# Dilated attention scores over 128 rows, h kept in DRAM meanwhile, three of eight probability units scaled on VectorE

## What is computed

```python
h = h + 0.5 * swiglu(rms_norm(h, ffn1_norm), ffn1_w1, ffn1_w3, ffn1_w2)
u = rms_norm(h, mix_norm)
proj = u @ w_in                       # q, k, v of 12 heads of 64; 4 pools; 2 gates
q, k = apply_partial_rope(q), apply_partial_rope(k)
for g, (window, dilation) in enumerate(((128, 1), (512, 4), (2048, 16))):   # 4 heads each
    s = (q @ k.T) * 64 ** -0.5        # banded, causal
    p = exp(s - max(s)); l = sum(p); o = p @ v / l; lse = max(s) + log(l)
o = sum(softmax(lse over the 3 groups) * o)
merged = gates[0] * (o @ w_branch_attn) + gates[1] * (pooled(proj) @ w_branch_pool)
h = h + merged @ w_out
h = h + 0.5 * swiglu(rms_norm(h, ffn2_norm), ...)      # then the retention and stick-breaking layers
```

## Time and profile before

| | |
|---|---|
| median of 3 runs | 1864.92 us (1864.58 to 1866.64) |
| profiled execution, its own time | 1866.13 us |
| span of that execution, first to last instruction | 1864.1 us |
| TensorE busy | 1850.0 us (99%), 10799 matmuls |
| weight loads (PEld) busy | 1627.6 us (87%) |
| VectorE busy | 1324.1 us (71%) |
| ACT busy | 890.8 us (48%) |
| POOL busy | 61.7 us (3%) |
| mean granted TensorE clock | 0.998 of full |
| DMA | 212.55 MB, mean 114 GB/s |

### The profile page before, as it was taken

One profiled execution on the slowest core, in us unless ns is written; L12 is line 12 of the kernel. 1 busy time (PEld: TensorE's weight loads), 2 busy tenths in 40 slices (PEclk: granted clock), 3 DMA queues, 4 the chain that ended last, 5 costly groups with the idle time before them and its releaser, 6 DMA issues.

```text
span 1864.1 us, 27146 instructions
## 1 busy us (share of the span) xinstructions
PE 1850.0 (99%) x10799; PEld 1627.6 (87%) x10799; DVE 1324.1 (71%) x1786; ACT 890.8 (48%) x1182; POOL 61.7 (3%) x80
## 2 busy tenths in 40 slices
PE   9999999999999999999999999999999999999997
PEld 7998998888889988989998888888888888888886
DVE  8875887887678889856888745463646776666666
ACT  6652664436365536634653342433336644444445
POOL 0000000010000000000000000000000000000000
PEclk9999999999999999999999999999999999999999
DMA  6744763341216426654753222122221222212213
GB/s 214 184 124 125 196 171 101 132 125 69 74 55 176 141 98 163 169 161 123 193 151 112 102 81 101 68 90 72 105 84 56 91 84 75 90 69 89 90 68 91
DMA packets 49633, 212.55 MB, mean 114 GB/s; under 512 B 5648, under 2 KB 8240, under 8 KB 38144
## 3 DMA queue, kind: packets, MB, share of 16 engines
q1 hardware_dynamic: 38816, 178.80, 28.1%
q0 software_dynamic: 10288, 31.84, 9.0%
q10 hardware_dynamic: 432, 0.56, 0.1%
HBM read 203.32 MB, written 3.67 MB: 111 GB/s over the span
## 4 chain that ended last, share of the span: by engine, by line
PE 94%; DVE 3%; ACT 1%; issue 1%; DMA 0%; DVEq 0%; ACTq 0%
PE acc L2419 20%; PE acc L2420 20%; PE acc L2421 20%; PE acc L2425 7%; PE acc L2426 7%; PE acc L2427 7%; PE att L2420 2%; PE att L2421 2%; PE att L2419 2%; PE att L2425 1%; PE att L2427 1%; PE att L2426 1%; PE acc L2683 1%; PE acc L2658 1%; DVE w_lo L1350 0%
## 5 line engine op out<-in xcount | busy, mean ns | idle before, releaser
L1350 DVE TENSOR_TENSOR w_lo<-raw,w_hi 128x2048 fp32r<-128x2048 f32 (+1 forms) x120 | 271.4, 2262 | 69.8 <-ACT w_hi L642 68.9
L642 ACT ACTIVATE w_hi<-raw 128x2048 fp32r<-128x2048 f32 (+1 forms) x120 | 226.5, 1888 | 120.4 <-PE acc L2421 105.6
L2419 PE MATMUL acc<-x_hi,w_hi 128*128 128x512 f32 x712 | 280.3, 394 | 0.3 <-DVE tmp L1578 0.3
L2421 PE MATMUL acc<-x_hi,w_lo 128*128 128x512 f32 x712 | 277.4, 390 | 0.0
L2420 PE MATMUL acc<-x_lo,w_hi 128*128 128x512 f32 x712 | 277.3, 389 | 0.0
L2419 PEld LDWEIGHTS acc<-x_hi,w_hi 128*128 128x128 f32 x712 | 133.7, 188 | 30.9 <-issue 2.7
L2420 PEld LDWEIGHTS acc<-x_lo,w_hi 128*128 128x128 f32 x712 | 133.7, 188 | 28.4 <-issue 1.2
L2421 PEld LDWEIGHTS acc<-x_hi,w_lo 128*128 128x128 f32 x712 | 133.6, 188 | 28.0
L2425 PE MATMUL acc<-xt_hi,w_hi 128*128 128x256 f32 x516 | 144.6, 280 | 0.0
L2427 PE MATMUL acc<-xt_hi,w_lo 128*128 128x256 f32 x516 | 144.3, 280 | 0.0
L2426 PE MATMUL acc<-xt_lo,w_hi 128*128 128x256 f32 x516 | 144.3, 280 | 0.0
(11 more groups left out here) (477 smaller groups left out, 4665.4 us busy)
## 6 DMA issues: line engine op xcount, KB each, us to landing
raw<-in_ret_head SPq DMA_DIRECT2D x24, 1024.0 KB, 4.8
raw<-in_ffn_down SPq DMA_DIRECT2D x32, 704.0 KB, 4.1
raw_c<-in_ffn_seven SPq DMA_DIRECT2D x37, 512.0 KB, 5.3
raw<-in_ffn_seven SPq DMA_DIRECT2D x33, 512.0 KB, 4.7
raw<-in_ffn_seven POOLq DMA_DIRECT2D x33, 512.0 KB, 7.5
raw<-in_ffn_seven SPq DMA_DIRECT2D x37, 256.0 KB, 4.5
raw<-in_ret_out SPq DMA_DIRECT2D x8, 1024.0 KB, 4.7
raw<-in_sb_v SPq DMA_DIRECT2D x8, 1024.0 KB, 4.7
```

Source lines behind the costliest of these rows:

```text
L642: nc.scalar.activation(w_hi[:, slot, at:at + cols], raw[:, slot, 0:cols], ACT.Copy).then_inc(w_hi_ready, 1)
L1350: tt(w_lo[:, slot, at:at + cols], raw[:, slot, 0:cols], w_hi[:, slot, at:at + cols].bitcast(F32), ALU.subtract).then_inc(w_ready, 1)
L2419: mm(dst, still[0], move[0], start=first, stop=False)
L2421: return mm(dst, still[1], move[0], start=False, stop=last)
```

## The change

`h` is written to a DRAM tensor `h_parked` by SP once the first feed-forward part has finished it, and is read back in four DMAs on Pool's queue behind the first four `add_pair`. In between, its room of 16 KB per partition holds `k_rest[j]` (per head j of the pass: low key parts of all groups on the head's own rows, zeros on the others) and `q_low[0]`, `q_low[1]`; `q_low[2]` takes the room of `ssq`. `q_both` and `k_both` now have all three groups; `qk_hi` and `qk_lo` are gone. Each group is copied in halves of 64 rows, and each has four DMAs to the other rows, twelve per pass. A unit has eight matmuls, all over 128 rows: the two masks, and two for each group. `first_score` waits for all twelve DMAs and for the zeros, VectorE's first low half for the store of h, and VectorE before adding to h for the four loads. VectorE no longer waits for the first pass's DMAs before the pool rows. For units 3, 5 and 7 VectorE multiplies by the reciprocal, right after taking it, and ACT doesn't.

```diff
+VECTOR_SCALED = (3, 5, 7)
...
+        with ExitStack() as under:
+            k_rest = [sb(f"k_rest{j}", [P, N_GROUPS, TOK], F32R, under) for j in range(2)]
+            q_low = [sb(f"q_low{g}", [P, TOK], F32R, under) for g in range(N_GROUPS - 1)]
         h = sb("h", [P, DC, TOK])
+        h_parked = nc.dram_tensor("h_parked", (P, DC, TOK), F32, kind="Internal").ap()
...
@@ SP
             for g in range(N_GROUPS):
                 fetch(dram["mix_qk"][0, g])
+            sp.wait_ge(h_ready, DC)
+            sp.dma_start(h_parked, h[:]).then_inc(park_landed, 16)
             for i in range(2):
                 fetch(dram["mix_pool"][i])
@@ POOL
+            pool.wait_ge(park_landed, 16)
+            pool.wait_ge(seg_done, FFN_SEGS[0] + 1)
+            for j, rows in enumerate(head_rows[::-1]):
+                nc.gpsimd.memset(k_rest[j][rows, :, :].bitcast(F32), 0.0).then_inc(rest_clear, 1)
...
+                for g in range(N_GROUPS):
+                    done = 2 * (N_GROUPS * a + g)
+                    pool.wait_ge(both_ready, done + 1)
+                    for j in range(2):
+                        pool.dma_start(q_both[j][other[j], g, :], q_low[g][own[j], :]).then_inc(both_landed, 16)
+                    pool.wait_ge(both_ready, done + 2)
+                    for j in range(2):
+                        pool.dma_start(k_both[j][other[j], g, :], k_both[j][own[j], g, :]).then_inc(both_landed, 16)
...
                     v.next()
+                    if j < 3:
+                        pool.wait_ge(prob_ready, 2 * UNITS)
+                        rows = slice(2 * (2 * (j - 1) + k), 2 * (2 * (j - 1) + k) + 2)
+                        pool.dma_start(h[:, rows, :], h_parked[:, rows, :]).then_inc(h_back, 16)
@@ ACT
-                if g:
-                    ins = nc.scalar.activation(qk_hi[:, o, g - 1, :], t(o), ACT.Copy, scale=QK_SCALE[o])
-                else:
-                    for j, rows in enumerate(head_rows):
-                        ins = nc.scalar.activation((k_both if o else q_both)[j][rows, :], t(o)[rows, :], ACT.Copy, scale=QK_SCALE[o])
+                for j, rows in enumerate(head_rows):
+                    ins = nc.scalar.activation((k_both if o else q_both)[j][rows, g, :], t(o)[rows, :], ACT.Copy, scale=QK_SCALE[o])
...
-                act.wait_ge(rden_ready, inv.next())
+                inv.next()
+                if k in VECTOR_SCALED:
+                    return
+                act.wait_ge(rden_ready, inv.k)
@@ VectorE
-                if g:
-                    stt(qk_lo[:, o, g - 1, :], t(o), QK_SCALE[o], qk_hi[:, o, g - 1, :].bitcast(F32), ALU.mult, ALU.subtract).then_inc(op_ready, 1)
-                else:
-                    for j, rows in enumerate(head_rows):
...
+                if both.k == 0:
+                    dve.wait_ge(park_landed, 16)
+                for j, rows in enumerate(head_rows):
+                    dst, high = (k_rest[j][rows, g, :], k_both[j][rows, g, :]) if o else (q_low[g][rows, :], q_both[j][rows, g, :])
+                    stt(dst, t(o)[rows, :], QK_SCALE[o], high.bitcast(F32),
+                        ALU.mult, ALU.subtract).then_inc(both_ready if j else op_ready, 1)
+                dve.wait_ge(both_ready, both.next())
...
                 nc.vector.reciprocal(rden[:, k:k + 1], den[:, k:k + 1]).then_inc(rden_ready, 1)
+                if k in VECTOR_SCALED:
+                    at = KEYS * (k % 3)
+                    dve.wait_ge(rden_ready, prob.k)
+                    nc.vector.tensor_scalar(tmp[:, at:at + KEYS], tmp[:, at:at + KEYS], rden[:, k:k + 1], None, ALU.mult).then_inc(vector_scaled, 1)
...
-            dve.wait_ge(both_landed, 4 * 16)
...
+            dve.wait_ge(h_back, 4 * 16)
@@ TensorE
-                mm(wide, both[:, plain[r]], keys[:], start=False, stop=False)
-                mm(wide, both[rows, plain[r]], k_low[rows, :], start=False, stop=True)
-                for g in range(N_GROUPS - 1):
-                    last = passes(narrow[:, P * g:P * (g + 1)], (q[0][:, g, :], q[1][:, g, :]),
-                                  (qk_hi[rows, 1, g, plain[r]], qk_lo[rows, 1, g, plain[r]]), False, g == N_GROUPS - 2)
+                q, high, rest = q_both[head], k_both[head], k_rest[head]
+                mm(wide, q[:, 0, plain[r]], high[:, 0, :], start=False, stop=False)
+                mm(wide, q[:, 0, plain[r]], rest[:, 0, :], start=False, stop=True)
+                for g in range(1, N_GROUPS):
+                    dst = narrow[:, P * (g - 1):P * g]
+                    mm(dst, q[:, g, plain[r]], high[:, g, plain[r]], start=False, stop=False)
+                    last = mm(dst, q[:, g, plain[r]], rest[:, g, plain[r]], start=False, stop=g == N_GROUPS - 1)
...
+                    if k in VECTOR_SCALED:
+                        pe.wait_ge(vector_scaled, by_vector.next())
+                    else:
+                        pe.wait_ge(scaled_ready, prob.next())
...
-                pe.wait_ge(both_landed, 4 * 16 * (a + 1))
+                pe.wait_ge(rest_clear, 2)
+                pe.wait_ge(both_landed, 4 * N_GROUPS * 16 * (a + 1))
```

More of the change, by code:

```diff
@@ L252, in block_kernel @@
             with ExitStack() as inner:
-                q_both = [sb(f"q_both{j}", [P, TOK], F32R, inner) for j in range(2)]
-                k_both = [sb(f"k_both{j}", [P, TOK], F32R, inner) for j in range(2)]
-                qk_hi = sb("qk_hi", [P, 2, N_GROUPS - 1, TOK], F32R, inner)
-                qk_lo = sb("qk_lo", [P, 2, N_GROUPS - 1, TOK], F32R, inner)
+                q_both = [sb(f"q_both{j}", [P, N_GROUPS, TOK], F32R, inner) for j in range(2)]
+                k_both = [sb(f"k_both{j}", [P, N_GROUPS, TOK], F32R, inner) for j in range(2)]
                 va = sb("va", [P, TB, N_GROUPS * GROUP_HEADS, 2, HEAD], F32R, inner)
@@ L408, in block_kernel @@
         both_landed = sem("both_landed")
+        park_landed = sem("park_landed")
+        rest_clear = sem("rest_clear")
+        h_back = sem("h_back")
         mix_copied = sem("mix_copied")
@@ L586, in _ @@
                 pool.dma_start(dst[:], dram[name]).then_inc(mix_landed, 16)
+            pool.wait_ge(park_landed, 16)
+            pool.wait_ge(seg_done, FFN_SEGS[0] + 1)
+            for j, rows in enumerate(head_rows[::-1]):
+                nc.gpsimd.memset(k_rest[j][rows, :, :].bitcast(F32), 0.0).then_inc(rest_clear, 1)
             def other_halves(a):
                 own, other = head_rows, head_rows[::-1]
-                pool.wait_ge(both_ready, 2 * a + 1)
-                for j in range(2):
-                    pool.dma_start(q_both[j][other[j], :], q_low[own[j], :]).then_inc(both_landed, 16)
-                pool.wait_ge(both_ready, 2 * a + 2)
-                for j in range(2):
-                    pool.dma_start(k_both[j][other[j], :], k_both[j][own[j], :]).then_inc(both_landed, 16)
+                for g in range(N_GROUPS):
[6 more added lines that the diff above has]
+                        pool.dma_start(k_both[j][other[j], g, :], k_both[j][own[j], g, :]).then_inc(both_landed, 16)
             other_halves(0)
@@ L1702, in rope_done @@
                 dve.wait_ge(hi_ready, hi.next())
-                if g:
-                    stt(qk_lo[:, o, g - 1, :], t(o), QK_SCALE[o], qk_hi[:, o, g - 1, :].bitcast(F32), ALU.mult, ALU.subtract).then_inc(op_ready, 1)
-                else:
-                    for j, rows in enumerate(head_rows):
-                        stt((k_low if o else q_low)[rows, :], t(o)[rows, :], QK_SCALE[o], (k_both if o else q_both)[j][rows, :].bitcast(F32),
-                            ALU.mult, ALU.subtract).then_inc(both_ready if j else op_ready, 1)
-                    dve.wait_ge(both_ready, both.next())
+                if both.k == 0:
[5 more added lines that the diff above has]
+                dve.wait_ge(both_ready, both.next())
                 op.next()
@@ L2631, in scores @@
             def scores(a, k):
-                r, rows = k // 2, slice(HEAD * (k % 2), HEAD * (k % 2) + HEAD)
+                r, head = divmod(k, 2)
                 if k >= 2:
```

11 lines of the change are left out of this document (3 added, 8 removed).

## The result

| | before | after |
|---|---|---|
| median of 4 runs | 1865.29 us (1864.58 to 1866.64) | 1882.55 us (1881.76 to 1883.38) |
| span of the profiled execution | 1864.1 us | 1881.6 us |
| TensorE busy | 1850.0 us | 1847.9 us |
| VectorE busy | 1324.1 us | 1334.1 us |

The changed kernel is slower: ratio 1.0092, 95% interval 1.0074 to 1.0109, or +17.3 us. 1875 with a range of 1868 to 1881 had been predicted: the sign was right, the size was not.

A forecast was written before the change was run, and what follows sets the result against it. TensorE, holding 94% of the chain, was taken to bound the kernel, with VectorE nearly abreast in the attention stage. Terms 4.0 - 0.6 + 8.9 - 1.2 - 0.9 = +10.2 us gave 1875 us, range 1868 to 1881.

The forecast's parts named there:

- the key transfers: Second pass, before the first score: both last-group key DMAs must land; two issues take 1.03 us, landing 2.3 us.
- first pass up to the first turn: Lengthened copies make TensorE 4.8 us later at the first value slab, two scores give back 0.8: +4.0 us.
- second pass up to the first score: Lengthened copies, then the last group's key DMAs, move the first score from 503.24 to 512.1: +8.9 us.
- rival a: Clock falls to 1.2 GHz in the wait before the second pass's first score: 3 to 5 us, 1877 to 1880; chance 0.3.
- The copies: Query and key copies of groups 1 and 2, halved: each 1.35 us longer, four times per pass over a head pair.
- the attend loops: VectorE decides the pace in each pass's loop: -0.6 us in the first, -0.9 in the second; bounds +0.3 and -2.0.
- The scaling: Attend loops, two of four rounds that split weights: VectorE takes 0.65 us per scaling, ACT gives up 0.83 us.
- The scores: TensorE saves 0.4 us a unit, at most 6.4 over 16 units; three before the second pass's first turn give -1.2.
- What was meant to be hidden: Store of h (6.7 us estimated), memsets and loads of h outside the attention stage's waits: priced at 0, to +1.5 us.
- (b): Copies shorter or better hidden, say by VectorE slack in the first pass: about +2.7 us, 1867.6; chance 0.14.
- (c): Scores count in full, everything else is covered by queued value blocks: -6.4 us, 1858.5; chance 0.05.
- (d): Scores over 128 rows of 128 columns take 0.2 us each, nothing saved: +13 us, 1878; chance 0.05.

The follow-up runs named there:

- e6_old_scores: Changed kernel with the ten score matmuls of before on the new tiles and all units scaled on ACT; 1884.53 us, ratio 1.0105.
- e2: Changed kernel with all eight units scaled on ACT again, none on VectorE; 1880.28 us, ratio 1.0080.
- e7_vector_halves: Kernel before with only VectorE's low parts of groups 1 and 2 in halves, ACT's copies whole; 1872.44 us, ratio 1.0035.
- e10b_early_keys: e8_reordered with each key transfer issued behind ACT's copy of its head instead of VectorE's last low part; 1874.23 us, ratio 1.0047.
- e8_reordered: Changed kernel, all scaling on ACT, scores of units 0 and 1 moved in both passes, useless matmuls before two rotations; 1874.30 us, ratio 1.0046.
- e1_keep_clock: Changed kernel with 53 useless matmuls in TensorE's four longest waits; 1878.41 us, ratio 1.0070.

## Why the prediction was wrong, step by step

Measured were +17.3 us instead of +10.2. Of the 7.1 us between them the clock is 4.1 to 4.5, the two attend loops 2.4 and the key transfers 0.4. The run with the clock kept shows the steps free of the clock, so its milestones are set against the terms of the sum.

| term | predicted | measured |
|---|---|---|
| first pass up to the first turn | +4.0 | +4.0 |
| loop of the first pass | -0.6 | +0.5 |
| second pass up to the first score | +8.9 | +9.3 |
| scores ahead of the first product | -1.2 | -1.2 |
| loop of the second pass | -0.9 | +0.4 |
| sum | +10.2 | +13.0 |
| clock | 0 (rival a: up to 5) | +4.1 of the medians, 4.5 between the two traces |

- **The copies: right.** The lengthenings of 1.35 us each gave 4.8 at the value slab, with 0.6 absorbed (measured 5.0), and 4.15 at the last rotation (measured 4.2). VectorE's halves alone gave half of that, and both engines' halves all of it. The +4.0 at the first turn was luck, though. I had TensorE arrive 4.8 later and win 0.8 by the scores; but filling TensorE's wait with scores moved nothing in the reordered kernel. With the clock kept, VectorE's weight split ahead of that turn starts 4.9 us later than before (430.88 instead of 425.97), and VectorE's idle time behind it shrinks from 2.31 us to 1.39: 4.9 less 0.9 is 4.0 as well. In the reordered kernel that idle time is 1.42. So the chain through VectorE's splits set the turn at the full clock; in the changed kernel, with the clock at 0.50, VectorE idled 3.07 us there, and TensorE set it.
- **The key transfers: right, 0.4 us too small.** I let the two issues follow at once (1.03 us for both the earlier trace rows); in the changed kernel they start 0.87 us apart instead of about 0.5:

```profile
516.36 0.52 POOL L609 DMA_DIRECT2D k_both<-k_both  x1 [5.17 <-DVE k_rest L1724]
517.23 0.52 POOL L609 DMA_DIRECT2D k_both<-k_both  x1 [0.35 <-issue]
```

- **The first step that failed: the attend loops** (-0.6 and -0.9 forecast, +0.5 and +0.4 measured). The prediction said "VectorE decides" and let its slip of 0.7 us be paid from the lead of the low part, 1.36 us. It also took the 3.01 us between two of VectorE's starts for its round; the round is 3.14 us long, and VectorE's work in it 2.86. Two errors weighed more. The lead of one product isn't what TensorE waits on most: its turn waits for the bank that VectorE's sum of the outputs frees (L2682 <- o_odd and o_even, 3.8 us in the waits), and the sum stands behind all of VectorE's round. So a round with a scaling is as long as VectorE's work in it: 3.50 us. And "ACT gives up 0.83 us" was read as a relief beside the bound, where ACT was itself the next bound: its round has 2.98 us of work against TensorE's 3.14, so new scores could shorten a round by at most 0.16 us, whatever TensorE saved. The trace of before had it. ACT, from the exp behind the scaling at 448.73 to the next scaling: only ahead of the rounding at 451.11 is there room, 0.16 us.

```profile
449.56 0.90 ACT L908 ACTIVATE tmp<-att,neg_max 128x768 f32<-128x768 f32 x1
450.34 0.21 ACT L908 ACTIVATION_READ_ACCUMULATOR tmp<-att,neg_max 128x1 f32 x1
450.43 0.64 ACT L652 ACTIVATE w_hi<-raw 128x512 fp32r<-128x512 f32 x1
451.11 0.60 ACT L931 ACTIVATE stage<-acc 128x512 fp32r<-128x512 f32 x1
451.61 0.38 ACT L933 ACTIVATE stage<-acc 128x256 fp32r<-128x256 f32 x1
451.87 0.94 ACT L916 ACTIVATE tmp<-tmp,rden 128x768 f32<-128x768 f32 x1
```

- **The scaling**, 0.62 us against 0.65 predicted: the size was right, its place was not. It costs 0.9 us a loop with the new scores, since it falls on two of four rounds and makes those 0.52 us longer (3.50 against 2.98), while the round between, where ACT doesn't scale, wins only 0.12 (2.86, VectorE's own work).
- **The scores**: 0.51 us a unit instead of 0.4; outside the loops they count nearly as forecast (0.9 and 1.3 us in the run with the scores alone, against 0.8 and 1.2). The reading that only the form of 64 rows shows a wait of 0.24 us for "issue" was wrong: 128-row weight loads show it too, in both kernels (464.65 us before, 471.51 after).
- **The second step that failed, and the larger: the clock.** It was a rival with chance 0.3, at one place, and in the forecast 0; measured 4.1 us. It fell at three places, because waits of 4.3 and 3.3 us, which the same prediction forecast for the value slab and the last rotation, were not put through the same question. 2.4 us of it came in the first pass, the rest in the second. The Trainium skill, page "TensorE: Matmul & The Clock Gate", section "Why this matters for your kernels", warned of idle gaps between bursts; the trace agrees in kind (clock 0.50 behind waits of 4.34, 3.30 and 4.25 us).
- **What was meant to be hidden, was**: the store of h (7.8 us to landing, 6.7 estimated), the memsets at 359.44, the loads of h, by the milestones of e6_old_scores.
- **The rivals.** (a) came true, in more places than it named, and on top of the two loops: 1875.1 + 4.1 + 2.4 + 0.4 = 1882.0, against 1882.55 measured. (b), (c) and (d) did not; (d) added up to too little as well, since it undid 2.7 us of the scores' gain and left out the 0.8 of the first pass. The range ended at 1881, as rival (a) reached 1880 with a fall of the clock in the second pass alone, and the loops' upper bound (+0.3 each) lay below what they came to (+0.5 and +0.4). That 1882.55 lies only 1.6 us above the range says little for the sum, which was 7 us off.

By parts, from the experiments: the halved copies +12.2; transfers and everything else of the new tiles +7.1 (1884.53 less 1865.28 of the runs of before beside it, less 12.2); the new scores -4.2 in that setting (e6 to e2), of which part is a shorter stretch at the low clock; the scaling +2.3, of which the loops show 1.9. These are steps from kernel to kernel, so they must add up to the whole; that they do is no test of them, and each step holds whatever the clock did in its two kernels.

## What to carry to other kernels

Before an engine is relieved or loaded inside a loop, add up each engine's work per round, for every kind of round: the gain ends at the next engine's sum, and a load shows wherever an engine's sum passes the bound, even if it does so in every second round only. A forecast wait of TensorE should be priced twice, once for itself and once for slow matmuls that may follow it, and each forecast wait must be asked that question. Where a transfer needs half of the rows, count the copies that are split for it: here they were the larger part of the price.

## What the runs showed of the hardware that I had not expected

- The granted clock fell from 2.4 to 1.2 GHz behind much shorter waits than I had priced, and not each time. It fell behind waits of 2.02 and 1.97 us (e7_vector_halves) and 1.97 us (e10b_early_keys, 0.66 in the window from 413 to 417); behind 1.91 us in e8_reordered it stayed at 1.00, and behind 1.34 us in e1_keep_clock too. In e6_old_scores it stayed at 1.00 even behind the last rotation's 3.3 us (1.00 in the window from 510 to 516).
- The stretch at the lower clock differs between like kernels: behind the same wait for the value slab about 7 us in the changed kernel and 3 to 4 in e6_old_scores. Executions of one kernel differ too: of the six of e7_vector_halves, the two with a mean granted clock of 0.998 took 1869.9 and 1870.2 us, the four with 0.996 or 0.997 took 1872.1 to 1873.5. That is not the whole scatter, since the kernel before scattered by 2 to 3 us at 0.998 or 0.999.
- A unit of eight matmuls over 128 rows takes 1.20 us against 1.71 for ten with seven of them over 64 rows, and no weight load within a unit waits 0.24 us for "issue" any more. The Trainium skill, page "TensorEngine Tiling (Array Packing)", section "Key Properties", says that changing the tiling mode drains TensorE; the rows fit that, as the wait stood once a unit, where the form of 64 rows began, but they don't show it, since waits of 0.24 us stand before 128-row loads too.
- VectorE's multiplication of 768 float32 columns by a per-row factor takes 620 ns, of 512 columns 486 ns, ACT's of 768 columns 940 ns: so a scaling takes a third less on VectorE, and it still cost time, as a round with it had no room on VectorE.
